# Three of four early keys summed on VectorE, a tree of adds for two reductions, and an earlier start of the selection

## What is computed

```python
def peer_ffn(h, wq, keys1, keys2, u_tab, v_tab):       # 8 heads, top 16 of 128 x 128 experts
    q = (ht @ wq).reshape(T, PEER_HEADS, 2, half)
    s1 = einsum('thd,kd->thk', q[:, :, 0], keys1)      # and s2 from q[:, :, 1], keys2
    v1, i1 = lax.top_k(s1, 16); v2, i2 = lax.top_k(s2, 16)
    cand = (v1[..., :, None] + v2[..., None, :]).reshape(T, 8, 256)
    cv, ci = lax.top_k(cand, 16)
    a = take_along_axis(i1, ci // 16); b = take_along_axis(i2, ci % 16)
    g = softmax(cv)
    act = gelu(einsum('thkd,td->thk', u_tab[a * 128 + b], ht))
    return einsum('thk,thkd->td', g * act, v_tab[a * 128 + b])
```

## Time and profile before

| | us |
|---|---|
| median of 3 runs | 2131.85 (2130.55 to 2134.74) |
| the profiled execution | 2129.88 |
| its span | 2127.6 |
| TensorE busy | 2115.6 (99%) |
| VectorE busy | 1236.7 (58%) |
| ScalarE busy | 1190.8 (56%) |
| GpSimd busy | 1705.0 (80%) |

### The profile page before, as it was taken

One profiled execution on the slowest core, in us unless ns is written; L12 is line 12 of the kernel. 1 busy time (PEld: TensorE's weight loads), 2 busy tenths in 40 slices (PEclk: granted clock), 3 DMA queues, 4 the chain that ended last, 5 costly groups with the idle time before them and its releaser, 6 DMA issues.

```text
span 2127.6 us, 48029 instructions
## 1 busy us (share of the span) xinstructions
PE 2115.6 (99%) x14294; PEld 1817.1 (85%) x14294; DVE 1236.7 (58%) x2509; ACT 1190.8 (56%) x2287; POOL 1705.0 (80%) x1316
## 2 busy tenths in 40 slices
PE   9999999999999999999999999999999999999999
PEld 7878899999888888888888788999988888888887
DVE  5756459876666555423357564598765665553233
ACT  5555665555555555555555566655555555545565
POOL 7766678988888888888897576789888888888887
PEclk9999999999999999999999999999999999999999
DMA  8433445555545554555574344455545454555555
GB/s 297 157 123 129 147 149 178 181 179 173 167 163 165 170 173 163 194 196 188 190 259 147 122 138 135 154 181 185 182 166 167 166 168 165 170 168 198 191 190 181
DMA packets 101789, 367.85 MB, mean 173 GB/s; under 512 B 11600, under 2 KB 12880, under 8 KB 101456
## 3 DMA queue, kind: packets, MB, share of 16 engines
q1 hardware_dynamic: 97632, 354.46, 50.2%
q10 hardware_dynamic: 4080, 12.42, 1.5%
HBM read 365.78 MB, written 1.05 MB: 172 GB/s over the span
## 4 chain that ended last, share of the span: by engine, by line
PE 97%; DVE 1%; ACT 1%; issue 1%; POOL 0%; ACTq 0%; DVEq 0%; POOLq 0%
PE acc L1243 17%; PE acc L1329 11%; PE acc L1331 11%; PE acc L1330 11%; PE acc L1242 7%; PE acc L999 6%; PE acc L1001 5%; PE acc L1000 5%; PE aux L1287 4%; PE acc L1235 3%; PE acc L1233 3%; PE acc L1234 3%; PE aux L932 2%; PE acc L1246 1%; PE aux L1110 1%; PE aux L1143 1%
## 5 line engine op out<-in xcount | busy, mean ns | idle before, releaser
L513 POOL TENSOR_TENSOR w_lo<-raw,w_hi 128x512 fp32r<-128x512 f32 x1312 | 1704.8, 1310 | 414.6 <-ACT w_hi L547 334.0
L547 ACT ACTIVATE w_hi<-raw 128x512 fp32r<-128x512 f32 x1348 | 843.5, 629 | 632.8 <-PE acc L1243 214.5
L1243 PE MATMUL acc<-h_rows,w_hi 128*128 128x512 f32 x1504 | 530.7, 397 | 0.0
L1329 PE MATMUL acc<-w_hi,eg 128*128 128x512 f32 x1020 | 401.0, 393 | 0.0
L1331 PE MATMUL acc<-w_hi,eg 128*128 128x512 f32 x1020 | 397.5, 390 | 0.0
L1330 PE MATMUL acc<-w_lo,eg 128*128 128x512 f32 x1020 | 397.0, 389 | 0.0
L2010 DVE TENSOR_TENSOR eg<-big,eg 128x256 fp32r<-128x256 f32 x256 | 149.6, 585 | 407.2 <-ACT eg L805 405.4
L1242 PE MATMUL acc<-h_rows,w_lo 128*128 128x256 f32 x1316 | 367.7, 279 | 0.0
L1243 PEld LDWEIGHTS acc<-h_rows,w_hi 128*128 128x128 f32 x1504 | 275.6, 188 | 50.9
L1242 PEld LDWEIGHTS acc<-h_rows,w_lo 128*128 128x128 f32 x1316 | 248.1, 189 | 8.4
L1331 PEld LDWEIGHTS acc<-w_hi,eg 128*128 128x128 f32 x1020 | 191.5, 188 | 40.7
(11 more groups left out here) (279 smaller groups left out, 2952.5 us busy)
## 6 DMA issues: line engine op xcount, KB each, us to landing
raw<-stream_dram SPq DMA_DIRECT2D x674, 512.0 KB, 3.3
big<-parb_dram ACTq DMA_DIRECT2D x2, 2128.0 KB, 9.8
big<-mem_dram ACTq DMA_DIRECT2D x2, 1024.0 KB, 5.2
big<-pm_dram ACTq DMA_DIRECT2D x2, 768.0 KB, 15.1
X<-x_dram ACTq DMA_DIRECT2D x1, 1024.0 KB, 7.9
out_dram<-X SPq DMA_DIRECT2D x4, 256.0 KB, 2.1
big<-parr_dram ACTq DMA_DIRECT2D x2, 448.0 KB, 11.6
big<-mem_dram ACTq DMA_DIRECT2D x1, 512.0 KB, 5.1
```

Source lines behind the costliest of these rows:

```text
L513: nc.gpsimd.tensor_tensor(w_lo[:, k % SLOTS, :], raw[:, k // PER_CHUNK, k % PER_CHUNK, :], w_hi[:, k % SLOTS, :].bitcast(F32), ALU.subtrac ...
L547: nc.scalar.activation(w_hi[:, k % SLOTS, :], raw[:, (k // PER_CHUNK) % RAW, k % PER_CHUNK, :], ACT.Copy).then_inc(hi_ready, 1)
L1243: ins = pe_.matmul(acc[:, bank_of, :], w_hi[:, r % SLOTS, at], h_rows[:, kt, :, :], start=(kt == 0), stop=(kt == KD - 1))
L1329: pe_.matmul(dst, eg[:, q % 2, 0, ts], w_hi[:, slot, :], start=start, stop=False)
```

## The change

It makes `SUMMED` (0, 1, 2), so 45 of the first 60 keys are of the `key_both` form, and `SPACING` 31. The scores of the second tile are copied only after head 1 of the first tile's selection, with the copy of `ranks` to PSUM behind them and a weight of 30. Each pair of reductions becomes four adds, three in place over 8, 4 and 2 of the 16 ranks, the last into `ab`, each with a weight of 8. The numbers of `u_sum` follow from `SUMMED`.

```diff
-SUMMED = (0, 2)
-SPACING = 47
+SUMMED = (0, 1, 2)
+SPACING = 31
...
-                sum_keys(2)
-                for t in range(T):
+                def read_scores(t):
+
                     for i in range(4):
                         use = f"ps{t}_{i}"
                         d.wait_filled(use)
                         d.step(V.tensor_scalar(rs[t][:, 4 * (i // 2):4 * (i // 2) + 4, i % 2, :],
                                                bank(use).rearrange("p (h k) -> p h k", h=4), ssx[:, t:t + 1], None, ALU.mult),
                                drains=use)
-                    if t == 0:
-                        sum_keys(4)
-                d.step(V.tensor_scalar(ranks_words, ranks.rearrange("p f j h -> p (f j h)").bitcast(U32), 0, None, ALU.bitwise_or))
+
+                sum_keys(2)
+                read_scores(0)
...
                             keys_between(19)
+                        if (t, h) == (0, 1):
+                            read_scores(1)
+                            d.step(V.tensor_scalar(ranks_words, ranks.rearrange("p f j h -> p (f j h)").bitcast(U32), 0, None,
+                                                   ALU.bitwise_or))
+                            keys_between(30)
...
-                    for f in range(2):
-                        d.step(V.tensor_reduce(ab[:, f, t].rearrange("p h k -> p k h"),
-                                               oh[:, f].rearrange("p j k h -> p k h j"), AX.X, ALU.add))
-                        keys_between(39)
+                    for n in (8, 4, 2):
+                        d.step(V.tensor_tensor(onehot[:, :, 0:n], onehot[:, :, 0:n], onehot[:, :, n:2 * n], ALU.add))
+                        keys_between(8)
+                    d.step(V.tensor_tensor(ab[:, :, t].rearrange("p f h k -> p f k h"), oh[:, :, 0], oh[:, :, 1], ALU.add))
+                    keys_between(8)
```

## The result

| | before | after |
|---|---|---|
| median, side by side | 2132.17 us (22 runs) | 2134.89 us (22 runs, 2132.99 to 2137.22) |
| ratio | | 1.0013, 95% interval 1.0007 to 1.0019 |
| the profiled execution, span | 2129.88, 2127.6 | 2133.57, 2131.7 |

The change costs 2.7 us, 1.5 to 4.1 by the interval: less than 0.2% of the time, but clear of zero by the interval.

The account below looks back on a forecast made before the run. TensorE, busy 2115.6 of 2127.6 us, was taken to bound the kernel. Per layer -0.9 us from TensorE and +1.9 of stops gave +2.0 for two layers, so 2133.9 us, range 2129.2 to 2138.5.

Parts of the forecast that it names:

- Adds and `w_lo` block each other: In the selection's tree, adds with two SBUF inputs and GpSimd's `w_lo` hold each other up; four adds take 6.6 us.
- Rival A: The adds pass beside GpSimd: tree 2.9 us, nothing late, 1.8 us faster, 2130.0 us; chance 0.18 together with D.
- rival B: The adds run at one element a cycle, twice the time; 4.65 us a layer lost, 2141.2 us; chance 0.15 with smaller forms.
- D: Adds and `w_lo` contend, but TensorE's feed takes more lateness than 2.5 us; time of Rival A, chance counted in its 0.18.
- Which sums are late: Behind the trees' adds, key 26's sum makes its gelu 2.5 us late in tile 0, key 50's 3.95 in tile 1.
- The limit of 2.5 us: A gelu on ScalarE may be some 2.5 us late for free; lateness beyond that stops TensorE.
- What the stops cost: TensorE's stops from the late gelus of keys 26 and 50: 0.2 and 1.7, together 1.9 us a layer.
- What TensorE gains: 15 more summed keys a layer save 0.06 us each on TensorE: 0.9 us a layer, 1.8 in all.
- Rival C: TensorE gains 4.5 us because neighbouring summed keys take 2.79 us; 2131.2 with stops, 2127.3 without; chance 0.10.
- The sum: Per layer -0.9 us from TensorE and +1.9 of stops, net +1.0; two layers +2.0.
- The early start worth nothing: Selection starts near 313.07 instead of 321.27, removing ScalarE's 2.41 us wait that TensorE never felt: worth nothing.
- The end of the stage with 6 us of slack: Slot weights are ready by 472.14, TensorE takes them at 478.23; 6 us cover the sums of keys 52 to 57.

## Why the prediction was right

The forecast was 2133.9, 2.05 above the three runs' median of 2131.85; measured were 2.7 more than before. Step by step:

- *Adds and `w_lo` block each other:* right, and shown. The first input in SBUF and the second in PSUM takes the blocking away. The tree of tile 0 took 390.34 - 384.01 = 6.33 us for 6.6 worked out; three adds of tile 1 took 5.08 for 5.05 (458.95 - 453.9). Rival A (2.9) and rival B (the first add over 3 us) fall by these rows, and D (a feed that takes more lateness) by the two stops.
- *Which sums are late:* right. The waits at keys 26 and 50 were 2.93 and 4.25 us for 2.5 and 3.95, about 0.4 and 0.3 more.
- *The limit of 2.5 us:* too high, and not one number. The gelus' waits less the stops' cost give 2.93 - 0.61 = 2.32 and 4.25 - 2.27 = 1.98, and with spacing 30 it is 2.50 - 0.22 = 2.28; with spacing 33 it goes from 1.3 to 3.5. The reading of the earlier trace rows wasn't wrong, but it is from a stretch of alternating keys. What it holds and what carries over is the way from the gelu to TensorE, 330.09 - 327.64 - 0.14 = 2.31 us there against 2.34 to 2.36 at the stops.
- *What the stops cost:* mis-sized, 1.9 us a layer taken (from the upper ends) and 2.88 measured. It is the same error seen from the other side: gelus 0.3 to 0.4 us later than worked out, and a limit lower by 0.2 and 0.5. The waits in the matmuls' rows (2.28) hide 0.6 of it; those of the weight loads show it.
- *What TensorE gains:* mis-sized the other way. I took 0.06 us a key from two neighbouring keys in the earlier trace rows. The stage without stops is 1.51 us shorter for its 14 converted keys, 0.11 each, 1.6 us a layer for 15 instead of 0.9. Over four keys it can be read without any experiment. Before, a key's first matmul and in the earlier trace rows the one four keys on (424.08):

```profile
412.69 0.28 PE L1233 MATMUL acc<-h_rows,w_hi 128*128 128x256 f32 x1
```

After, the same matmul of keys 35 and 39:

```profile
407.78 0.28 PE L1233 MATMUL acc<-h_rows,w_hi 128*128 128x256 f32 x1
...
419.05 0.28 PE L1233 MATMUL acc<-h_rows,w_hi 128*128 128x256 f32 x1
```

  It is 11.39 us against 11.27, 0.12 for the one key of four that changed its form. Rival C's mechanism was therefore partly true: 3.0 to 3.2 us in all, between my 1.8 and its 4.5. With stops of 2.88 us a layer it can't be seen in the total.
- *The sum:* -1.5 + 2.9 = +1.4 a layer in place of -0.9 + 1.9 = +1.0. Two terms were off by 0.6 and 1.0 us and mostly cancelled. That the total came out 0.7 us from the measurement is partly luck.
- *The early start worth nothing:* wrong as a step for itself. It removes no felt wait, as I wrote, but it keeps the selection ahead of its sums, and without it the change costs 3.2 us more. The sum held because I had worked out the lateness of keys 26 and 50 from the new start.
- *The end of the stage with 6 us of slack:* true of the weights' last operation, and blind to the tighter thing there. The gelu of key 54 has next to no play ahead of the table load. In the kernel after it was in time. The selection did end earlier, as forecast: VectorE's subtraction ends 142.7 us after key 4 for 146.5 before. It buys nothing, for ScalarE's load starts in its order, 1.4 us later than before.
- The rule of the Trainium skill (SBUF — State Buffer, section "Who interferes with whom") that the second to issue is blocked agrees with the rows: the first adds wait for the running `w_lo` (1287 ns), and the next `w_lo` is stretched to 2197. The other rule of the Trainium skill here (TensorE: Matmul & The Clock Gate, section "Wait — 56ns, not 53.3ns?"), 2.5 ns a matmul, would give an estimated 0.02 us for the 8 matmuls of a key. The trace has 0.11, 14 ns a matmul.

## What to carry to other kernels

When work of one engine is placed by hand into a stream that another engine waits for, compute for each placement how late its result comes and how late it may come, and put the results that are due ahead of the long operations. Here the same instructions took from 2129.5 to 2145 us as one spacing constant went from 30 to 33, and no operation saved was worth as much. The play has to be read where it is used: 2.0 to 2.3 us at three gelus in the middle of the stage, and about none ahead of ScalarE's table load. It is better counted back from the time at which TensorE needs the result, here some 2.35 us, than read from a wait. A gain per step is read over a whole period of the pattern, and a stop of TensorE from the waits of its weight loads.

## What was not expected of the hardware

- Short VectorE operations with both inputs in SBUF can cost far more than their own time beside a busy GpSimd: in the kernel after the 512-element add took 1.39 us or more where 0.42 is its own time, and the last add 1.59 where it is 0.61. Each waits for the 1.3-us operation that runs. With GpSimd idle the last add took 0.60. Whether one pass over more elements would be blocked only once was not tested.
- A stop of TensorE on `w_lo` cost 0.23 us beyond the 0.38 that its matmul's row shows, and 0.37 beyond 1.90. The rows of the weight loads show 0.69 and 2.21, within 0.1 us of the cost.
- A smaller number of matmuls for the same columns saved 14 ns for each one left out.
- Gelus that waited 2.50 and 2.19 us lengthened the stage by some 0.2 us each without a wait in any matmul's row; two weight loads' waits of 0.22 us show it, and so do the starts of the keys, laid beside those of another kernel.
